# A hybrid decoder layer on one core: the next head's scores are formed ahead of the current head's value products

## The reference, cut to what matters

```python
(q_a, kvc, kvs, kvw, g_nsa, q_b, f_b, i_b, og_b, g_mrg) = jnp.split(h @ w_in, splits, axis=-1)
...
s_c = jnp.einsum('btghd,bngd->btghn', qg, ck) * NSA_SCALE - slopes * dist_c
p_c = masked_softmax(s_c, (dist_c >= 0))
o_cmp = jnp.einsum('btghn,bngd->btghd', p_c, cv)
...
s = jnp.einsum('btghd,bgtnsd->bgthns', qg, gath[..., 0, :]) * NSA_SCALE - slopes * dist
p = masked_softmax(s, dist >= 0)
o_sel = jnp.einsum('bgthk,bgtkd->btghd', p, gath[..., 1, :])
... # o_win likewise, over the window's keys
o = g[..., 0:1] * o_cmp + g[..., 1:2] * o_sel + g[..., 2:3] * o_win
...
ga, gb = jnp.split(g_mrg, 2, axis=-1)
mixed = (sigmoid(ga) * (o_a @ w_a) + sigmoid(gb) * (o_hg @ w_b)) @ w_o
```

## Time and profile before

| | |
|---|---|
| median of 3 runs | 2108.43 us (2103.07 to 2110.52) |
| the profiled execution's own time | 2107.65 us |
| its span, first to last instruction | 2105.8 us |
| TensorE busy, share of the span | 2000.6 us, 95% |
| VectorE | 1039.7 us, 49% |
| ScalarE | 861.4 us, 41% |
| GpSimd | 142.1 us, 7% |
| mean granted TensorE clock | 0.981 |

### The profile page before, as it was taken

How to read it: one execution, slowest core, us unless ns; L and a number is a source line. 1 busy time by engine, 2 the same in 40 slices (tenths; PEclk the granted TensorE clock), 3 DMA queues, 4 the chain that set the end, 5 groups by cost and what they waited for, 6 DMA issues and landing times. The chain is left out here.

```text
span 2105.8 us, 34893 instructions
## 1 busy us (share of the span) xinstructions
PE 2000.6 (95%) x13539; PEld 1942.8 (92%) x13539; DVE 1039.7 (49%) x1564; ACT 861.4 (41%) x1270; POOL 142.1 (7%) x215
## 2 busy tenths in 40 slices
PE   5999999998999999999988999999999999999896
PEld 4999988898899999999986999999999999999895
DVE  3322453332466666554347555533555543455465
ACT  5331454332334434443335444422454432345443
POOL 2420200221000000100000000000000000000000
PEclk9999999999999999999998999999999999999998
DMA  7898534667455554667551555555555555555452
GB/s 205 198 271 207 139 100 111 179 170 237 124 134 151 141 150 127 190 191 209 154 157 41 155 144 151 148 142 157 141 158 140 155 144 144 155 145 154 115 143 86
DMA packets 534852, 324.60 MB, mean 154 GB/s; under 512 B 9169, under 2 KB 523650, under 8 KB 534008
## 3 DMA queue, kind: packets, MB, share of 16 engines
q1 hardware_dynamic: 517184, 272.12, 48.7%
q0 software_dynamic: 12304, 45.49, 7.2%
q10 hardware_dynamic: 5288, 5.94, 0.8%
HBM read 305.01 MB, written 22.04 MB: 155 GB/s over the span
## 5 line engine op out<-in xcount | busy, mean ns | idle before, releaser
L1051 DVE TENSOR_TENSOR wlo<-raw,whi 128x2048 fp32r<-128x2048 f32 x252 | 577.7, 2292 | 864.8 <-ACT whi L614 864.8
L1520 PE MATMUL ps<-hH,whi 128*128 128x320 f32 x2752 | 873.4, 317 | 13.8 <-DVE hL L1071 5.3
L1520 PE MATMUL ps<-hH,wlo 128*128 128x320 f32 x2752 | 855.4, 311 | 0.0
L1520 PE MATMUL ps<-hL,whi 128*128 128x320 f32 x2752 | 855.4, 311 | 0.0
L614 ACT ACTIVATE whi<-raw 128x2048 fp32r<-128x2048 f32 x253 | 484.0, 1913 | 689.8 <-PE ps L1520 614.1
L1520 PEld LDWEIGHTS ps<-hH,whi 128*128 128x128 f32 x2752 | 522.3, 190 | 27.7 <-issue 17.7
L1520 PEld LDWEIGHTS ps<-hL,whi 128*128 128x128 f32 x2752 | 522.3, 190 | 0.9
L1520 PEld LDWEIGHTS ps<-hH,wlo 128*128 128x128 f32 x2752 | 521.3, 189 | 0.0
L1520 PE MATMUL ps<-aH,whi 128*128 128x320 f32 x704 | 218.2, 310 | 2.7 <-DVE aL L1464 2.7
L1520 PE MATMUL ps<-aL,whi 128*128 128x320 f32 x704 | 217.8, 309 | 0.0
L1520 PE MATMUL ps<-aH,wlo 128*128 128x320 f32 x704 | 217.7, 309 | 0.0
(11 more groups left out here) (294 smaller groups left out, 1790.9 us busy)
## 6 DMA issues: line engine op xcount, KB each, us to landing
raw<-in_w_up SPq DMA_DIRECT2D x88, 1024.0 KB, 5.7
raw<-in_w_in SPq DMA_DIRECT2D x85, 1024.0 KB, 5.7
raw<-in_w_down SPq DMA_DIRECT2D x32, 1024.0 KB, 5.8
raw<-in_w_out SPq DMA_DIRECT2D x16, 1024.0 KB, 5.8
raw<-in_w_down SPq DMA_DIRECT2D x16, 768.0 KB, 5.0
w_buf<-in_cmp_w SPq DMA_DIRECT2D x32, 256.0 KB, 5.8
raw<-in_w_branch_a SPq DMA_DIRECT2D x16, 512.0 KB, 4.2
raw<-in_w_branch_b SPq DMA_DIRECT2D x16, 512.0 KB, 5.4
```

Of the source, the lines that this page charges most:

```text
L1051: TT(wlo[:, slot], raw[:, slot], whi[:, slot].bitcast(F32), ALU.subtract).then_inc(lo_ready, 1)
L1520: ins = pe.matmul(out, ww[:, slot, w, :], xx[:, k, :], start=(start and q == 0 and p_ == 0), stop=(stop and q == last and p_ == 2), skip_g ...
```

## The change

Three lists are written in another order; no instruction is added or removed.

On **TensorE** the scores of head h + 1 now come straight behind the transposes of head h, and the value products of head h come behind them. The gate unit is cut into 4, 8 and 4 blocks (it was 12 and 4). For heads 1 to 7 the first two pieces follow one another; only for head 0 do its scores stand between them. On **VectorE** `scored` of head h + 1 now comes ahead of the split `wlo` and of `oL` of head h. On **ScalarE** the scaled queries of the next pair come ahead of the copies `pT` and `pTc`, where they came behind them.

```diff
@@ ScalarE
                         for qt in range(2):
                             exps(h * 2 + qt, qt * PW, (qt + 1) * P, (qt + 1) * P)
+                        if par and h < HEADS - 1:
+                            scaled_q(t + 2 * g + 1)
                         for qt in range(2):
                             act.wait_ge(pt_ps, h * 2 + (qt + 1))
...
                             act.activation(pTc[0:NCMP, qt, :], ps[0:NCMP, 7, 0:P], ACT.Copy).then_inc(pt_ok, 1)
-                        if par and h < HEADS - 1:
-                            scaled_q(t + 2 * g + 1)
                         gate_step(par, t + 2 * g)
@@ VectorE
+            def head_low(h):
+                dve.wait_ge(oh_ok, h + 1)
+                TT(oL[:, ds(h, 1), 0:SEQ], ps[:, 0:1, 0:SEQ], oH[:, ds(h, 1), 0:SEQ].bitcast(F32), ALU.subtract
+                   ).then_inc(ol_ok, 1)
+
+            def head_scored(h):
+                for qt in range(2):
...
+            head_scored(0)
+            for h in range(HEADS):
+                for qt in range(2):
+                    weighted(h * 2 + qt, qt * PW, (qt + 1) * P, gate_p[:, qt, 3 * h:3 * h + 3])
+                if h < HEADS - 1:
+                    head_scored(h + 1)
+                gate_step(h % 2, h // 2)
+                head_low(h)
@@ TensorE
+            FIRST, SECOND = 4, 12
+
             def merge_gate(par, m, part=0, n=N_MG, bank=None):
...
-                tiles = (all16, all16[:12], all16[12:])[part]
+                k0, k1 = ((0, KT), (0, FIRST), (FIRST, SECOND), (SECOND, KT))[part]
...
+            def head_values(h):
+                g = h // HPG
+                if h:
+                    pe.wait_ge(ol_ok, h)
+                for qt in range(2):
+                    pe.wait_ge(pt_ok, h * 2 + (qt + 1))
...
+                ins.then_inc(ov_ps, 1)
+
+            for h in range(HEADS):
+                par, m = h % 2, h // 2
+                if h == 0:
+                    merge_gate(par, m, 1)
+                    scores(h)
+                    merge_gate(par, m, 2)
+                else:
+                    head_values(h - 1)
+                    merge_gate(par, m, 1)
+                    merge_gate(par, m, 2)
+                turned_probs(h, 0)
+                merge_gate(par, m, 3)
+                turned_probs(h, 1)
+                if h < HEADS - 1:
+                    scores(h + 1)
+            head_values(HEADS - 1)
```

More of the change, by code:

```diff
@@ L1156, in weighted @@
                         ins.then_inc(pn_ok, 1)
[L1158 to L1176, removed]
+            def head_low(h):
[4 more added lines that the diff above has]
+                for qt in range(2):
+                    nk = (qt + 1) * P
+                    off = P if qt == 0 else 0
+                    scored(h * 2 + qt, qt * PW, nk,
+                           ps[:, 2 + qt, 0:2 * nk].rearrange("p (b k) -> p b k", b=2),
+                           bias_p[:, h:h + 1, off:off + nk].to_broadcast([P, 2, nk]),
+                           ps[:, 4, qt * NCMP:(qt + 1) * NCMP], bias_pc[:, qt, h, :])
+            head_scored(0)
[6 more added lines that the diff above has]
+                head_low(h)
             def sample_out(k):
@@ L1644, in merge_gate @@
                     pe.wait_ge(gs_rd[par], m)
-                tiles = (all16, all16[:12], all16[12:])[part]
+                k0, k1 = ((0, KT), (0, FIRST), (FIRST, SECOND), (SECOND, KT))[part]
                 gemm(m * 2 + (n + par), (N_MG + par) % 2, ps[:, 1 + 4 * par if bank is None else bank, 0:T], hH, hL,
-                     tiles, wait=(part < 2), done=(part != 1), start=(part < 2), stop=(part != 1))
+                     all16[k0:k1], wait=(k0 == 0), done=(k1 == KT), start=(k0 == 0), stop=(k1 == KT))
@@ L1650, in _ @@
             PW = 512 + NCMP
[L1651 to L1688, removed]
@@ new lines, in scores @@
+            def scores(h):
+                g, par = h // HPG, h % 2
+                pe.wait_ge(q_ok, h + 1)
+                if h:
+                    pe.wait_ge(sc_rd, h * 2)
+                for qt in range(2):
+                    product(ps[:, 4, qt * NCMP:(qt + 1) * NCMP], qst[:, par, qt * P:qt * P + P], ckT[:])
+                for qt in range(2):
+                    nk = (qt + 1) * P
+                    q = qst[:, par, qt * P:qt * P + P]
+                    product(ps[:, 2 + qt, 0:nk], q, kvq[:, 4 + g, 0:nk])
+                    product(ps[:, 2 + qt, nk:2 * nk], q, kvq[:, 8 + g, 0:nk]).then_inc(sc_ps, 1)
@@ new lines, in turned_probs @@
+            def turned_probs(h, qt):
+                base, nb = qt * PW, 2 * (qt + 1)
+                pe.wait_ge(pn_ok, h * 2 + (qt + 1))
+                if h * 2 + qt:
+                    pe.wait_ge(pt_ok, h * 2 + qt)
+                for b in range(nb):
+                    pe.transpose(ps[:, 6, b * P:b * P + P], prob[:, base + b * P:base + b * P + P], ident)
+                pe.transpose(ps[0:NCMP, 7, 0:P], prob[:, base + nb * P:base + nb * P + NCMP], ident
+                             ).then_inc(pt_ps, 1)
@@ new lines, in head_values @@
+            def head_values(h):
+                g = h // HPG
+                if h:
+                    pe.wait_ge(ol_ok, h)
+                for qt in range(2):
+                    pe.wait_ge(pt_ok, h * 2 + (qt + 1))
+                    out = ps[:, 0, qt * P:qt * P + P]
+                    for br, col in enumerate((6 + g, 10 + g)):
+                        for kt in range(qt + 1):
+                            product(out, kvtok[:, kt, col * P:col * P + P], pT[qt][:, br * (qt + 1) + kt, :],
+                                    start=(br == 0 and kt == 0), stop=False)
+                    ins = product(out, cv[0:NCMP, :], pTc[0:NCMP, qt, :], start=False)
+                ins.then_inc(ov_ps, 1)
```

## The result

The changed kernel took 2096.38 us (median of 5 runs, 2095.93 to 2100.44) against 2108.82 us before (median of 5, 2103.07 to 2110.52). The ratio is 0.9949, with a 95% interval from 0.9931 to 0.9966: 10.8 us less, between 7.2 and 14.5. A second series of the changed kernel gave 0.9965 (0.9952 to 0.9978). The forecast of 8.85 us, a ratio of 0.9958, lies in both intervals.

A forecast was written before the change was run, and what follows sets the result against it. TensorE, busy 95% of the span, bounds the kernel, with waits from a loop through VectorE's split. Waits of 5.9 and 2.6 us plus 0.35 at the start make 8.85: 2107.65 to 2098.8, forecast 2099 us, 8 in 10 within 2094 to 2106.

The forecast's parts named there:

- The two waits and their sum: TensorE's waits at the transposes (probabilities, 5.9 us) and value products (copies, 2.6 us) go; with 0.35 us earlier start, 8.85 us.
- The start: Start of the stage: first 4 gate blocks need only the copy kvq, so TensorE begins about 0.35 us earlier (0 to 0.4).
- The chain on VectorE and ScalarE: One head's turn: scores, split, oL, exponentials and weighting finish 1.5 and 2.3 us before TensorE wants the probabilities.
- The first rival: VectorE reads scores only near 3.8 us, holding the split; seven heads lose 6.3 of 8.85 us: 2105 us, chance 0.14.
- The places with little to spare: Transposes after head 4's 16 small copies, 0.4 us left, cost at most 0.3; head 0, 0.6 us left.
- Scaled queries: ScalarE's 8 copies move to where it waits for transposes anyway, no longer ahead of whi in each second head.
- The time beyond the stage: The sample stage and what follows hang on this stage's end through semaphores and should move forward as a whole.
- the third rival: TensorE's clock: one slow stretch, costing 1.7 us, more or fewer gives 2101 or 2097 us; no chance of its own.
- The second rival: Near 499 to 513 us a weight load meets the window's whole copy; wait grows up to 10.9 us: 2110, chance 0.06.
- The fourth rival: TensorE meets other waits of the same length, for oL or the gate weights; no change, 2107 us, chance 0.04.

The follow-up runs named there:

- the second experiment: Kernel before with VectorE's new order alone, TensorE and ScalarE as before: ratio to before 0.9970 (0.9957 to 0.9983), 6.3 us less.
- the fourth experiment: Changed kernel with the gate unit cut into 4, 4 and 8 blocks: ratio to before 0.9978 (0.9961 to 0.9994).
- The third experiment: Changed kernel with the scaled queries put back behind the copies pT and pTc: ratio to before 0.9974 (0.9960 to 0.9987).
- the first four experiments: Changed kernel with VectorE's old order (0.9981); before with VectorE's new order alone (0.9970); changed kernel with queries put back (0.9974), or gate unit 4, 4, 8 (0.9978).

## Why the prediction was right, step by step

**The two waits and their sum.** Waits for probabilities 5.9 us and copies 2.6 us were to go, and the start was to come 0.35 us earlier. All seven waits for probabilities went, seven of the eight for copies went, and that of head 7 stayed with its 0.37 us. The turn is 11.46 us where 11.48 was worked out. The start was the term that was off: TensorE began at 231.66, not near 231.45, 0.14 us earlier than before, and the stop there shrank from 3.02 to 2.82 us only. ScalarE's copy was through at 231.02 + 0.42 = 231.44, about as foreseen; the prediction let TensorE start 0.06 us behind it, and it started 0.22 behind:

```profile
231.02 0.42 ACT L669 ACTIVATE kvq<-ps 128x320 f32<-128x320 f32 x1
```

Together it is 8.89 us against 8.85. That the two agree to 0.04 us is luck: up to the end of head 0's transposes (243.12 before, 242.88 in the changed kernel) 0.24 us was gained, 0.11 less than the 0.35 for the start, and the seven turns gave 8.64, 0.14 more than the 5.9 + 2.6 for the waits.

**The chain on VectorE and ScalarE.** From the transposes at 265.81 the scores were read at 1.20 (1.3 expected) and done at 3.69 (3.7), the split ran from 3.80 (3.80), oL from 6.01 (6.0), the weighting of qt 0 ended at 7.40 (7.4), and TensorE wanted it at 8.79 (8.90). On ScalarE, oH began at 3.85 (3.85):

```profile
269.66 0.39 ACT L779 ACTIVATE oH<-ps 128x256 fp32r<-128x256 f32 x1
```

The first rival, in which the scores come too late and hold the split, is what happens when TensorE keeps its old order: the second experiment. ScalarE's row in the turn of that experiment shows the high part through at 257.63 + 1.91 = 259.54:

```profile
257.63 1.91 ACT L614 ACTIVATE whi<-raw 128x2048 fp32r<-128x2048 f32 x1 [0.50 <-ACT mgate L714]
```

VectorE began the split at 260.96, 1.4 us later, since the scores stood ahead of it. The Trainium skill, "TensorE: Matmul & The Clock Gate", section on the 16 sub-arrays, calls VectorE's queue strict first-in first-out; the trace agrees: VectorE took all eight score instructions first, although the split's input was there 1.4 us before they were through.

**The places with little to spare.** Head 5 was expected to have 0.4 us and had about 0.7, head 0 was expected to have 0.6 and had about 0.3, both by the fourth experiment. Neither made a wait in the changed kernel.

**Scaled queries.** The prediction called their move free and did not say that the new order on TensorE needs it. The third experiment shows 4.2 us of waits without it.

**The time beyond the stage.** The profiled span fell by 7.2 us, not 8.9. The price of the third rival shows itself there: one more stretch at 1.2 GHz. ScalarE's first copy of the transposed probabilities in the sample stage, and its copy in the next part of that stage, before:

```profile
356.94 0.38 ACT L809 ACTIVATE pTs<-ps 128x256 f32<-128x256 f32 x1 [5.92 <-PE ps L1727]
...
384.50 0.59 ACT L802 ACTIVATE KTs<-ps 128x512 f32<-128x512 f32 x1
```

and in the changed kernel:

```profile
348.07 0.38 ACT L809 ACTIVATE pTs<-ps 128x256 f32<-128x256 f32 x1 [5.14 <-PE ps L1748]
...
377.14 0.59 ACT L802 ACTIVATE KTs<-ps 128x512 f32<-128x512 f32 x1
```

The first is 8.87 us earlier, the second 7.36. Between them TensorE's weight loads stop for the same 1.49 us, before:

```profile
358.13 0.52 PEld L1511 LDWEIGHTS ps<-kvtok,pTs 64*128 64x128 f32 x4 [1.49 <-ACT pTs L813]
```

and in the changed kernel:

```profile
349.26 0.52 PEld L1515 LDWEIGHTS ps<-kvtok,pTs 64*128 64x128 f32 x4 [1.49 <-ACT pTs L813]
```

In the changed kernel the granted clock fell behind it:

```profile
350.00:352.00 2.00, 2.00 (x36) 1.65 (x37) 0.05 (x1) 2.00 (x2) 0.00 (x0) 0.81 0.23 82
352.00:354.00 2.00, 2.00 (x9) 2.00 (x9) 2.00 (x1) 0.08 (x1) 0.72 (x1) 0.50 0.04 12
354.00:356.00 2.00, 2.00 (x13) 2.00 (x12) 0.24 (x1) 0.00 (x0) 1.43 (x2) 0.84 0.44 95
```

The stretch of before that answers to the second of these, some 9 us later, had 1.00:

```profile
360.00:362.00 2.00, 2.00 (x24) 1.80 (x13) 1.19 (x1) 0.94 (x2) 0.48 (x1) 1.00 0.03 8
```

But the new order is not shown to be the cause. In the second profile of the changed kernel the weight loads stop at the same place for the same 1.49 us, the clock stays up, and the two copies lie 27.56 us apart, as before (384.50 - 356.94); in the first profile it was 29.07:

```profile
349.03 0.38 ACT L809 ACTIVATE pTs<-ps 128x256 f32<-128x256 f32 x1 [5.91 <-PE ps L1748]
...
376.59 0.59 ACT L802 ACTIVATE KTs<-ps 128x512 f32<-128x512 f32 x1
```

```profile
352.00:354.00 2.00, 2.00 (x28) 1.80 (x16) 1.10 (x1) 1.04 (x2) 0.40 (x1) 1.00 0.03 8
```

**The second rival**, the copy of the window's state, did not come: the wait for the weight load is 14.60 us against 14.22, the copy lands after 25.4 us against 25.1.

```profile
506.33 1.91 ACT L614 ACTIVATE whi<-raw 128x2048 fp32r<-128x2048 f32 x1 [14.60 <-DMA raw<-in_w_in]
```

```profile
out<-in_state_win_kv POOLq DMA_DIRECT2D x1, 3968.0 KB, 25.4
```

**The fourth rival** did not come either: in the turn shown TensorE has no wait for `oL` or for the gate weights.

What stays open is the last few microseconds of the times. Behind the stage the eight profiles (before, the changed kernel twice, five variants) have the same code, and it took from 1769.3 us (the queries put back) to 1774.8 us (TensorE's and ScalarE's order without VectorE's). The time at 1.2 GHz between 330 and 2070 us, added up from stretches of 2 us (one between 0.50 and 1.00 counts in proportion), was 51 us in the first of these and 68 us in the last, and between 58 and 65 in the other six; the changed kernel's first profile had 65 us and 1773.3, its second 61 us and 1771.3. More time at 1.2 GHz goes with a longer rest, but no run changed the clock alone.

The times of the runs say the same. Of the 34 runs of the kernel before that stand beside the first four experiments, the fastest, 2099.48 us, had a mean granted clock of 0.984 and the slowest, 2115.70 us, 0.974; over all 34 the correlation of time and clock is -0.88. The two ratios of the changed kernel, 0.9949 and 0.9965, both have 0.9958 in their intervals and need no cause beyond this spread.

## What to carry to other kernels

When an engine at 95% waits for a chain through others, write out one turn from a common zero and find which instruction of the chain stands behind unrelated work in its engine's list; moving that one is worth its wait. Move all lists of the chain together: here VectorE's list alone gave 4.5 us of the stage, TensorE's and ScalarE's without it 1.8, all three 8.8, and the small copies of the queries left in their old place took back 4.1. The gain of such a move ends at the bound engine's own work, here the 11.46 us of a turn, so look next for the stops at the ends of the stage, where the clock may be lost as well.

## What the runs showed that was not expected

A stop of 0.96 us left TensorE's clock at 2.4 GHz, and the stops of 2.82 to 3.02 us at the same place were followed by 1.2 GHz in all seven other profiles. The stop of 1.49 us in the sample stage was followed by 1.2 GHz in three of the eight profiles (the changed kernel's first, VectorE's order alone, the gate unit cut into 4, 4 and 8) and not in the other five, among them the changed kernel's second. So that stop has no fixed price.
